# When ScalarE copies eight transposed tiles out of PSUM at the head of an MLP

## The reference

```python
def _sqrelu_mlp(h, w1, w2):          # w1: 1024 x 4096, w2: 4096 x 1024
    u = jax.nn.relu(h @ w1)
    return (u * u) @ w2
...
    for i in range(DEPTH_2):         # 2 layers: retention, then chunk attention
        hn = _rmsnorm(h, mix_norm_g[i])
        ...
        h = h + _sqrelu_mlp(_rmsnorm(h, mlp_norm_g[i]), mlp_w1[i], mlp_w2[i])
```

## Time and profile before

| | |
|---|---|
| median of 3 runs | 1976.07 us (1975.45 to 1976.45) |
| the profiled execution's own time | 1975.45 us |
| its span | 1973.7 us |
| PE busy | 1927.0 us, 98% |
| DVE busy | 1328.8 us, 67% |
| ACT busy | 976.5 us, 49% |
| mean granted clock of TensorE | 0.998 |

### The profile page before, as it was taken

One profiled execution on the slowest core, in us unless ns is written; L12 is line 12 of the kernel. 1 busy time (PEld: TensorE's weight loads), 2 busy tenths in 40 slices (PEclk: granted clock), 3 DMA queues, 4 the chain that ended last, 5 costly groups with the idle time before them and its releaser, 6 DMA issues.

```text
span 1973.7 us, 25953 instructions
## 1 busy us (share of the span) xinstructions
PE 1927.0 (98%) x10236; PEld 1639.0 (83%) x10236; DVE 1328.8 (67%) x1807; ACT 976.5 (49%) x1392; POOL 642.5 (33%) x456
## 2 busy tenths in 40 slices
PE   8999999999999999999999999999999999999997
PEld 7877878888888888888888798988888888798896
DVE  7667753433267855555558888889566778888888
ACT  7445442322244452525256564656455557464665
POOL 2433545554545435353533011110333342101010
PEclk9999999999999999999999999999999999999999
DMA  5312367376232313231314546575322233646554
GB/s 163 94 44 75 109 88 120 101 106 117 87 103 89 107 67 104 66 105 64 106 64 128 150 150 171 129 192 129 105 85 85 85 91 103 191 122 188 123 157 126
DMA packets 166220, 221.46 MB, mean 112 GB/s; under 512 B 4512, under 2 KB 119968, under 8 KB 165984
## 3 DMA queue, kind: packets, MB, share of 16 engines
q1 hardware_dynamic: 151600, 190.52, 29.7%
q0 software_dynamic: 12928, 25.71, 7.6%
q10 hardware_dynamic: 1584, 3.74, 4.2%
HBM read 214.84 MB, written 4.72 MB: 111 GB/s over the span
## 4 chain that ended last, share of the span: by engine, by line
PE 62%; DVE 21%; ACT 8%; issue 7%; POOL 1%; DMA 1%; DVEq 0%; SPq 0%; ACTq 0%; POOLq 0%
PE ps L1045 19%; PE ps L1046 19%; PE ps L1047 19%; DVE w_lo L3262 6%; DVE hid_lo L3277 2%; DVE o_buf L3400 2%; ACT w_hi L1759 2%; ACT x L2371 2%; PE ps L1217 1%; ACT x L2373 1%; PE ps L1247 1%; POOL w_lo L929 1%; DVE scr L2617 1%; DVE x L3357 1%; ACT hid_hi L2385 1%
## 5 line engine op out<-in xcount | busy, mean ns | idle before, releaser
L929 POOL TENSOR_TENSOR w_lo<-raw,w_hi 128x512 fp32r<-128x512 f32 x376 | 530.6, 1442 | 667.6 <-ACT w_hi L1753 667.6
L1045 PE MATMUL ps<-hn_hi,w_hi 128*128 128x512 f32 (+1 forms) x1524 | 555.6, 365 | 7.3 <-ACT o_buf L2325 4.6
L1047 PE MATMUL ps<-hn_hi,w_lo 128*128 128x512 f32 (+1 forms) x1524 | 546.8, 359 | 0.0
L1046 PE MATMUL ps<-hn_lo,w_hi 128*128 128x512 f32 (+1 forms) x1524 | 546.6, 359 | 0.0
L1045 PEld LDWEIGHTS ps<-hn_hi,w_hi 128*128 128x128 f32 x1524 | 288.9, 190 | 55.2 <-ACT o_buf L2325 5.4
L1753 ACT ACTIVATE w_hi<-raw 128x2048 fp32r<-128x2048 f32 (+1 forms) x98 | 186.0, 1898 | 287.1 <-PE ps L1047 287.0
L1047 PEld LDWEIGHTS ps<-hn_hi,w_lo 128*128 128x128 f32 x1524 | 288.7, 189 | 42.9
L1046 PEld LDWEIGHTS ps<-hn_lo,w_hi 128*128 128x128 f32 x1524 | 289.0, 190 | 41.4 <-issue 1.7
L1045 PE MATMUL ps<-w_hi,hid_hi 128*128 128x512 f32 x456 | 180.6, 396 | 22.6 <-DVE w_lo L3262 9.4
L1046 PE MATMUL ps<-hid_lo,w_hi 128*128 128x512 f32 (+1 forms) x504 | 184.3, 366 | 0.0
L1045 PE MATMUL ps<-hid_hi,w_hi 128*128 128x512 f32 (+1 forms) x488 | 179.5, 368 | 0.1
(11 more groups left out here) (396 smaller groups left out, 3436.3 us busy)
## 6 DMA issues: line engine op xcount, KB each, us to landing
raw<-in_mlp_w SPq DMA_DIRECT2D x50, 1024.0 KB, 5.3
raw<-in_ret_w_in SPq DMA_DIRECT2D x24, 1024.0 KB, 5.1
aux<-in_mlp_w POOLq DMA_DIRECT2D x16, 1024.0 KB, 8.4
unit_raw<-in_mlp_w SPq DMA_DIRECT2D x14, 1024.0 KB, 6.6
raw<-in_att_w_in SPq DMA_DIRECT2D x12, 1024.0 KB, 5.3
raw<-in_w_gate SPq DMA_DIRECT2D x11, 1024.0 KB, 5.4
raw<-in_w_up SPq DMA_DIRECT2D x11, 1024.0 KB, 5.3
raw<-in_w_down SPq DMA_DIRECT2D x8, 1024.0 KB, 8.2
```

The source lines that it names most:

```text
L929: ins = pool.tensor_tensor(w_lo[:, slot, at], raw[:, slot, at], w_hi[:, slot, at].bitcast(F32), ALU.subtract)
L1045: pe.matmul(o, hi, rhs_hi, start=start, stop=False, skip_group_check=True)
L1046: pe.matmul(o, hi, rhs_lo, start=False, stop=False, skip_group_check=True)
L1047: return pe.matmul(o, lo, rhs_hi, start=False, stop=stop, skip_group_check=True)
```

## The change

In `first_group` of ScalarE the same instructions are issued in another order. The copies of tiles 0 to 4 and 5 to 7 come later, the high parts of A12, T2 and T1 earlier; nothing is added and nothing removed. As the function serves both MLPs, the order changes in both places.

```diff
                     gained_b12()
-                    token_copy(0)
                     act.wait_ge(s["mlp_sum"], ml.first_sums(SUM[T3]))
                     first_t(T3, t3_raw)
-                    token_copy(1)
                     unit_hi(ml, 0, 1, ml.U_A11)
-                    token_copy(2)
+                    unit_hi(ml, 0, 1, ml.U_A12)
                     act.wait_ge(s["mlp_sum"], ml.first_sums(SUM[T2]))
                     first_t(T2, t2_raw, -1.0)
-                    token_copy(3)
-                    unit_hi(ml, 0, 1, ml.U_A12)
-                    token_copy(4)
                     act.wait_ge(s["mlp_sum"], ml.first_sums(SUM[T1]))
                     act.wait_ge(s["norm_acc"], norm.acc0 + norm.added)
                     first_t(T1, t1_raw)
-                    token_copy(5)
+                    token_copy(0)
+                    token_copy(1)
                     plain_squared(0)
-                    token_copy(6)
+                    token_copy(2)
+                    token_copy(3)
                     r_for_tokens()
+                    token_copy(4)
                     unit_hi(ml, 0, 1, ml.U_S3)
-                    token_copy(7)
+                    for f in range(5, KD):
+                        token_copy(f)
                     unit_hi(ml, 0, 1, ml.U_M)
                     plain_squared(1)
```

## The result

The changed kernel takes 1986.61 us (median of 5, 1985.52 to 1987.01) against 1976.07 us: 10.5 us more, ratio 1.0051 with a 95% interval of 1.0037 to 1.0066. The forecast was 1982.5 us with a range of 1979.2 to 1985.5. The sign is right, the size is not.

A forecast was written before the change was run, and what follows sets the result against it. TensorE was taken as the bound nearly everywhere, VectorE's and ScalarE's chain as setting A21. Two places, each 1.7 us excess shift plus 1.5 us clock loss, gave 6.4 us over 1976.07: 1982.5 us, range 1979.2 to 1985.5.

The forecast's parts named there:

- the copies serve TensorE and the moved high parts gain nothing: High parts of A12, T2, T1 serve VectorE, which isn't waiting for ScalarE: no gain; TensorE's tile 3 needs copy 0.
- The shift of 5.66 us at tile 3: Tile 3's transposes wait for copy 0, moving TensorE's work from step 3 on from 1062.77 to 1068.43, 5.66 us.
- The slack of 3.9 us: TensorE's waits before A11, M and A21 together: a smaller delay from the second plain product costs nothing, a greater its excess.
- forecast 1.7: Excess of TensorE's shift over its slack up to A21: 1.76 us a place, taken as 1.7.
- the excess lasts to the end: Behind A21 the wait at 1109.69 (1.51 us) moves along with TensorE's own earlier result and absorbs none of the excess.
- I take one, 1.5 us: Clock loss behind each place's new wait: one half-clock stretch of 3.41 us, costing 1.5 us a place.
- a fall at both places: TensorE's clock falls behind the new wait of about 5.5 us at both places; no fall 0.08, one fall 0.08.
- The upper bound, 3.0 us a place: Most the clock was taken to cost behind each new wait: two half-clock stretches, 3.0 us.
- the rival that the clock stays low twice as long: Clock loss behind each new wait of 3.0 us: 9.4 us slower in all, 1985.5 us; chance 0.09.
- S3's weight part still near 1073.65: ScalarE's weight part of S3 stays at 1073.65, set by VectorE; copy 4 after a slow step 4 pushes it under 1 us.

The follow-up runs named there:

- copy0_first: The changed kernel with only copy 0 put back ahead of T3; 1977.45 us against 1976.43 for the kernel before, ratio 1.0004.
- copy7_early: The kernel before with only copy 7 moved ahead of the weight part of S3; 1977.4 us against 1976.43, ratio 1.0008.
- fill24: The changed kernel with 24 more matmuls of 512 columns ahead of the wait for tile 3, both places; 1979.88 us against 1976.43 for the kernel before.

## Why the prediction was wrong in size

- **That the copies serve TensorE and the moved high parts gain nothing**: right. VectorE's stretch is unchanged, and copy 0 started at 1067.80 on the old scale.
- **The shift of 5.66 us at tile 3**: right, 5.5 us of wait shown, tile 3 within 0.01 us of the forecast.
- **The slack of 3.9 us**: right. Less than that costs nothing while the clock stays up (copy0_first, second place of copy7_early), and beyond it the excess is paid: 1.62 us a place in fill24, forecast 1.7.
- **That the excess lasts to the end**: right; 5.2 + 5.0 us between tile 2 and A21 against 10.5 in the time.
- **The clock, "I take one, 1.5 us"**: this is the step that failed. It took the low clock behind the new wait to last as long as behind the old one, 3.41 us. It lasted 10.24 us in the first trace and 6.83 in the second, 7.3 to 7.7 and 5.9 to 6.4 of them with TensorE busy, and cost 3.6 and 3.4 us in the first and 2.75 and 3.0 in the second. 2 x (1.7 + 3.5) = 10.4 us gives the result. The mechanism, a fall at both places, was right, and the size was taken from the only fall that the trace of before showed, one behind a wait less than half as long. The upper bound, 3.0 us a place, was two such stretches, and it too was short; the rival that the clock stays low twice as long, given 0.09, came nearest.
- **"S3's weight part still near 1073.65"**: wrong, 1.55 us late, since copy 4 ahead of it waited for the slowed step 4. The forecast had named this with under 1 us; it cost nothing, as it had said, since TensorE was later still. Part of the delay was even given back, which the forecast had not seen: the low part of S3's weights (1076.93) now starts after GpSimd's addition has ended (1074.35 + 2.37 = 1076.72) and takes 1.23 us in place of 2.39.

Why the clock falls 2.5 us into one wait and 5.1 us into another of the same length, in one and the same program, stays open. What is shown is that it is low for 6.8 or 10.2 us behind 5.5 us of idle time (seven of seven places), for nothing (five), 3.4 us (seven) or 6.8 us (one) behind 2.3 to 2.9 us, and not at all when the idle time is filled. The rule of the Trainium skill that the prediction weighed ("TensorE: Matmul & The Clock Gate", section "HAM oscillation — how this bites in real kernels"), that a long enough wait between bursts puts the array back to its slow clock each time, held at all seven places with 5.5 us; that a wait of 2.3 us or less can do so as well is what the traces add.

## What to carry to other kernels

A copy out of a PSUM bank that is one of few is work for the engine that refills the bank, however idle that engine looks at the end of the stretch: before moving it, add up from the trace when the next tile wants the bank, and how much slack lies behind that point until the chains meet again. A wait of TensorE that exceeds the slack is paid twice, once as idle time and once as a lower clock behind it, and here the second was the larger; a fall seen behind a short wait is no upper bound for a long one. And look for the slow instance of an operation on the engine that does set the path: its neighbour on another engine may be free to run later.

## What the runs showed of the hardware

- Behind a wait of 5.5 us TensorE's granted clock was at 1.2 GHz for 6.8 us (four places) or 10.2 us (three), the part inside the wait counted in; the same program showed both, and the falls that came 2.5 to 3.3 us into the wait were the long ones, those at 3.8 to 5.1 us the short ones. Of thirteen places with a wait of 2.3 to 2.9 us in the traces of seven kernels, five showed no fall, seven one of 3.4 us and one of 6.8. The shortest wait with a fall behind it was 1.74 us, at one of four such places.
- Behind the waits of 5.5 us where TensorE set the path, the fall cost half of the low time in which TensorE was busy, less 0.2 to 0.3 us (7.3 to 8.1 us of it cost 3.4 to 3.8; 5.9 to 6.4 us cost 2.75 to 3.0).
- 24 matmuls into an unused bank during the wait kept the clock up and won 2.75 to 3.6 us a place against the two traces of the changed kernel, though their results are thrown away.
- A VectorE operation on 128x1024 float32 with two inputs, which alone takes 1.22 us, and a GpSimd addition of the same shape, which alone takes 2.37 us, did not run side by side at full pace: the one that started second took longer by about what was left of the first. VectorE's took 2.39 us where it started 1.04 us after GpSimd's and 1.76 where it started 1.73 us after it, and ended 1.08 us after it both times. In a later group of the kernel before it is the other way round: VectorE starts at 1138.44 and takes its 1.22 us, GpSimd starts at 1138.61 and takes 3.31.
